# Layer 1 attention with one merged score block per unit, and its masked copies made by GpSimd

## The reference, cut to what matters

```python
qi = jnp.arange(WINDOW)[:, None] + WINDOW
kj = jnp.arange(2 * WINDOW)[None, :]
rel = qi - kj
valid = ((rel >= 0) & (rel < WINDOW))[None] & ((jnp.arange(nb)[:, None, None] > 0) | (kj[None] >= WINDOW))
scores = jnp.where(valid[None, :, None, None], scores, -jnp.inf)
m = jnp.maximum(jnp.max(scores, axis=-1), sink)
p = jnp.exp(scores - m[..., None])
denom = jnp.sum(p, axis=-1) + jnp.exp(sink - m)
o = jnp.einsum('bnhgqk,bnkhd->bnhgqd', p, vv.astype(F32)) / denom[..., None]
```

## Time and profile before

| | us |
|---|---|
| median of 3 runs | 2116.43 (2115.18 to 2119.19) |
| span of the profiled execution | 2115.3 |
| mean granted TensorE clock | 0.990 |
| busy: PE | 2045.7 (97%) |
| busy: DVE, ACT, POOL | 1604.8, 1361.3, 277.7 |
| stretch of the attention units | about 1226 to 1462 |

### The profile page before, as it was taken

How to read it: one execution, slowest core, us unless ns; L and a number is a source line. 1 busy time by engine, 2 the same in 40 slices (tenths; PEclk the granted TensorE clock), 3 DMA queues, 4 the chain that set the end, 5 groups by cost and what they waited for, 6 DMA issues and landing times. The chain is left out here.

```text
span 2115.3 us, 30221 instructions
## 1 busy us (share of the span) xinstructions
PE 2045.7 (97%) x10536; PEld 1661.4 (79%) x10536; DVE 1604.8 (76%) x2000; ACT 1361.3 (64%) x1794; POOL 277.7 (13%) x334
## 2 busy tenths in 40 slices
PE   8999998998999999999999989999899999999998
PEld 6888876787788888888877856777688888888885
DVE  4551246777888888888886267887898888888886
ACT  5333426653788887878772266675577778888774
POOL 2000000001111121111203320110111111122210
PEclk9999999999999999999999999999999999999999
DMA  4112222215999999999983020011699999999996
GB/s 139 40 60 90 78 72 78 81 65 205 343 381 390 389 389 385 380 378 380 385 317 132 1 90 11 21 61 61 231 383 380 381 384 384 387 388 385 384 363 254
DMA packets 123491, 513.28 MB, mean 243 GB/s; under 512 B 27373, under 2 KB 28490, under 8 KB 89610
## 3 DMA queue, kind: packets, MB, share of 16 engines
q1 hardware_dynamic: 103674, 474.11, 59.7%
q0 software_dynamic: 18576, 33.86, 4.2%
q10 hardware_dynamic: 1152, 4.19, 0.5%
HBM read 495.05 MB, written 50.86 MB: 258 GB/s over the span
## 5 line engine op out<-in xcount | busy, mean ns | idle before, releaser
L542 DVE TENSOR_TENSOR exp_w_lo<-ring_raw,first_w_hi 128x2048 fp32r<-128x2048 f32 x192 | 438.9, 2288 | 33.2 <-ACT first_w_hi L469 33.1
L542 DVE TENSOR_TENSOR exp_w_lo<-ring_raw,exp_w_hi 128x2048 fp32r<-128x2048 f32 x192 | 438.8, 2287 | 27.8 <-ACT exp_w_hi L469 27.8
L469 ACT ACTIVATE exp_w_hi<-ring_raw 128x2048 fp32r<-128x2048 f32 x192 | 367.7, 1918 | 62.1 <-PE exp_up_out L394 27.9
L469 ACT ACTIVATE first_w_hi<-ring_raw 128x2048 fp32r<-128x2048 f32 x188 | 360.7, 1919 | 62.2 <-PE exp_up_out L394 23.6
L339 POOL DMA_INDIRECT y_rows<-exp_y,base_rows_y x63 | 79.8, 1266 | 936.1 <-ACT exp_y L489 936.1
L394 PE MATMUL exp_gate_out<-exp_w_lo,exp_x_hi 128*128 128x512 f32 x512 | 201.1, 393 | 0.0
L394 PE MATMUL exp_y_out<-exp_w_lo,exp_hid_hi 128*128 128x512 f32 x512 | 200.4, 391 | 0.0
L394 PE MATMUL exp_up_out<-exp_w_lo,exp_x_hi 128*128 128x512 f32 x512 | 199.3, 389 | 0.0
L546 DVE TENSOR_TENSOR exp_x_lo<-exp_x_turned,exp_x_hi 128x1024 fp32r<-128x1024 f32 x62 | 75.9, 1224 | 51.4 <-ACT exp_x_hi L473 51.4
L394 PE MATMUL exp_gate_out<-first_w_hi,exp_x_hi 128*128 128x512 f32 x272 | 109.7, 403 | 3.1 <-issue 2.0
L350 POOL DMA_INDIRECT first_x_rows<-u_rows,base_rows_u x64 | 104.9, 1639 | 58.6 <-issue 52.2
(11 more groups left out here) (529 smaller groups left out, 4671.8 us busy)
## 6 DMA issues: line engine op xcount, KB each, us to landing
ring_raw<-in_expert_w_gate_dram SPq DMA_DIRECT2D x128, 1024.0 KB, 11.1
ring_raw<-in_expert_w_up_dram SPq DMA_DIRECT2D x128, 1024.0 KB, 11.6
ring_raw<-in_expert_w_down_dram SPq DMA_DIRECT2D x128, 1024.0 KB, 11.4
l0w_raw<-in_ab_w_in_dram SPq DMA_DIRECT2D x48, 256.0 KB, 2.8
finish_y<-y_rows SPq DMA_DIRECT2D x8, 1024.0 KB, 12.4
ring_raw<-in_swa_w_qkv_dram SPq DMA_DIRECT2D x5, 1024.0 KB, 10.1
ring_raw<-y_rows SPq DMA_DIRECT2D x10, 512.0 KB, 4.9
base_h<-in_x_dram ACTq DMA_DIRECT2D x8, 512.0 KB, 7.0
```

The lines of the kernel that those rows point to most:

```text
L469: nc.scalar.activation(split[split_slot(unit)][0][:], raw[raw_slot(unit)][:], ACT.Copy).then_inc(hi_ready, 1)
L542: nc.vector.tensor_tensor(lo[:], raw[raw_slot(unit)][:], hi[:].bitcast(F32), ALU.subtract).then_inc(lo_ready[split_slot(unit)], 1)
```

## The change

1. **One block of scores.** For n >= 1 ACT copies the own block's scores to `masked` (`copy_own`), and DVE overwrites the places k > q with the previous block's scores by a predicated copy. Each query so has 128 scores, not 256. Maxima, exponents and both normalizations work on 128 columns a head. For n = 0 DVE still adds a mask.
2. **Four transposes.** `turn(G)` transposes 4 blocks instead of 8; `turned` has two halves, used in turn.
3. **A copy and two masked copies.** `copy_turned(G)` writes 512 columns to `bare` in SBUF. GpSimd multiplies them by the two triangles in `band` into the two halves of `prob_t` (`band_probs(G)`, previous first), and `weigh(G)` waits for these. The wait for `out_ready` moves from ACT to GpSimd.
4. **Order.** `units` puts one output unit ahead of each turn and three behind it. On ACT `copy_own(G + 2)` comes first in a pass and `norm_even(G + 1)` right behind `copy_turned(G)`. On DVE `denominators(G + 1)` comes before `mask(G + 2)`. On GpSimd `rotate(7)`, the router's multiply and the inverse roots stand between the `band_probs`.

```diff
+            def band_probs(G):
+                pool.wait_ge(s["bare_copied"], G + 1)
+                if G >= 1:
+                    pool.wait_ge(s["out_ready"], G)
+                for b in range(0 if G >= GROUPS else 1, 2):
+                    g.tensor_tensor(by_head(prob_t[:, b * BANK:(b + 1) * BANK]), by_head(bare[G % 3]), bc(c["band"][:, b], 1, PER), ALU.mult).then_inc(s["own_made" if b else "prev_made"], 1)
...
-            for u in range(T - 2):
-                inverse_root(u)
+            for G in range(LAST):
+                band_probs(G)
+                if G == 0:
+                    rotate(T - 1)
+                    pool.wait_ge(s["router_ready"], 32)
+                    g.tensor_tensor(router[:], router[:], bc(c["ffn_gain1"], 2, 36), ALU.mult).then_inc(s["router_scaled"], 1)
+                if G % GROUPS == 0 and G >= 2 * GROUPS:
+                    inverse_root(G // GROUPS - 2)
...
-                p_of = heads4(masked[G % 3])
-                for b in range(0 if n else 1, 2):
-                    if b == 0 and G > GROUPS:
-                        pe.wait_ge(s["early_copied"], G - GROUPS)
-                    if b == 1 and G > 0:
-                        pe.wait_ge(s["prob_copied"], G)
-                    for i in range(PER):
-                        last = nc.tensor.transpose(turned[:, PER * b + i], p_of[:, i, b], c["ident"][:])
-                    last.then_inc(s["prob_turned" if b else "early_turned"], 1)
+                if G > 1:
+                    pe.wait_ge(s["bare_copied"], G - 1)
+                for i in range(PER):
+                    last = nc.tensor.transpose(turned_at(G)[:, i], by_head(masked[G % 3])[:, i], c["ident"][:])
+                last.then_inc(s["prob_turned"], 1)
...
                     if b == 0:
-                        pe.wait_ge(s["early_copied"], G - GROUPS + 1)
+                        pe.wait_ge(s["prev_made"], G - GROUPS + 1)
                     else:
-                        pe.wait_ge(s["prob_copied"], G + 1)
+                        pe.wait_ge(s["own_made"], G + 1)
...
-            units = {(0, 0): (0, 3), (0, 1): (3, 4), (1, 0): (4, 7), (1, 1): (7, 8), (2, 0): (8, 9), (2, 1): (9, 10), (3, 0): (10, 14), (3, 1): (14, 16)}
+            units = {(0, 0): (0, 1), (0, 1): (1, 4), (1, 0): (4, 5), (1, 1): (5, 8), (2, 0): (8, 9), (2, 1): (9, 12), (3, 0): (12, 13), (3, 1): (13, 16)}
...
+            def copy_own(G):
+                act.wait_ge(s["scored"], G + 1)
+                act.wait_ge(s["prob_turned"], G - 2)
+                a.activation(by_head(masked[G % 3]), heads4(scores)[:, :, 1], ACT.Copy).then_inc(s["own_copied"], 1)
+
             def copy_turned(G):
-                if G >= 1:
-                    act.wait_ge(s["out_ready"], G)
...
+                act.wait_ge(s["prob_turned"], G + 1)
+                if G >= 3:
+                    act.wait_ge(s["own_made"], G - 2)
+                a.activation(by_head(bare[G % 3]), turned_at(G), ACT.Copy).then_inc(s["bare_copied"], 1)
...
+                    dve.wait_ge(s["own_copied"], G - GROUPS + 1)
+                    v.copy_predicated(by_head(masked[j]), bc(c["tri_strict"][:].bitcast(U32), 1, PER), heads4(scores)[:, :, 0]).then_inc(s["masked_made"], 1)
```

More of the change, by code:

```diff
@@ L2297, in layer1 @@
         q_cols, prob_t = [chunks(work[j][:]) for j in range(2)], work[2][:]
-        masked = [work[n][:] for n in (3, 4, 5)]
+        masked, bare = [work[n][:, 0:BANK] for n in (3, 4, 5)], [work[n][:, BANK:] for n in (3, 4, 5)]
+        turned_at = lambda G: turned[:, PER * (G % 2):PER * (G % 2 + 1)]
         r_rows = [q[:, t + 2, 0:1024] for t in range(5)] + [raw_ring[4][:, 0:1024], late[:, 1], late[:, 2]]
@@ L2824, in exponents @@
             def exponents(G):
-                j, first = G % 3, 0 if G >= GROUPS else P
+                j = G % 3
                 act.wait_ge(s["tops_made"], G + 1)
                 for i in range(PER):
-                    span = slice(i * 2 * P + first, (i + 1) * 2 * P)
-                    a.activation(masked[j][:, span], masked[j][:, span], ACT.Exp, bias=neg_top[j][:, i:i + 1], accum_out=total[j][:, i:i + 1])
+                    own = by_head(masked[j])[:, i]
+                    a.activation(own, own, ACT.Exp, bias=neg_top[j][:, i:i + 1], scale=HEAD_DIM ** -0.5, accum_out=total[j][:, i:i + 1])
@@ L2830, in exponents @@
                 a.activation(sink_part[j][:], sink_part[j][:], ACT.Exp).then_inc(s["prob_made"], 1)
             def norm_even(G):
-                j, first = G % 3, 0 if G >= GROUPS else P
+                j = G % 3
                 act.wait_ge(s["inv_made"], G + 1)
                 for i in range(2):
-                    span = slice(i * 2 * P + first, (i + 1) * 2 * P)
-                    last = a.activation(masked[j][:, span], masked[j][:, span], ACT.Copy, scale=inv[j][:, i:i + 1])
+                    own = by_head(masked[j])[:, i]
+                    last = a.activation(own, own, ACT.Copy, scale=inv[j][:, i:i + 1])
@@ L3023, in denominators @@
                 for i in range(2, PER):
-                    span = slice(i * 2 * P + first, (i + 1) * 2 * P)
-                    last = v.tensor_scalar(masked[j][:, span], masked[j][:, span], inv[j][:, i:i + 1], None, ALU.mult)
+                    own = by_head(masked[j])[:, i]
+                    last = v.tensor_scalar(own, own, inv[j][:, i:i + 1], None, ALU.mult)
                 last.then_inc(s["odd_normed"], 1)
```

56 lines of the change are left out of this document (24 added, 32 removed).

## The result

The changed kernel takes 2182.52 us in the median (2179.62 to 2187.34), the kernel before on the same chip 2117.26. The ratio is 1.0306, with a 95% interval of 1.0293 to 1.0319: slower by 65 us, where 2173 us was forecast, with 2140 to 2200 as the range. The profiled execution spans 2177.9 us against 2115.3, so 62.6 us are to be found. Of all executions on record one, of experiment 7, ran in a slow state and took 3930 us; it is left out of the ratios but not out of that kernel's median.

What follows compares the result with a forecast made beforehand. PE was taken to bound the kernel before, the chain through ACT and GpSimd the changed one. Terms 31 + 2.6 + 3 + 2 + 12 + 6 = 57 us on 2115.3 gave 2172, plus 1.1 against the median 2173 us; range 2140 to 2200.

Steps and rivals of the forecast that it cites:

- (a): On PE: four transposes fewer a unit, 0.39 us each in 28 units, 11 us in all while PE bounds.
- (b): Chain from one weighing to the next through ACT and GpSimd's pair: 6.9 us in an ordinary unit.
- (c): Units of a block from n = 2 on: 7.4, 11.6, 8.9 and 6.9 us, together 31 us more for five blocks.
- (d): Other units: +2.6 us for units 4 to 8, +3 for n = 0, +2 for the last block.
- (e): PE's clock falls after the long waits in g = 1, slowing the next stretch: 0 to 18 us, +12 taken.
- (f): SBUF port shared by DVE and GpSimd: instructions hold each other, +6 us, with 0 and 25 as ends.
- PE stays the bound: Rival: both masked copies done 2.6 us after the turn, so PE gains its 11 us; 2108 us, chance 4 in 100.
- Only the inverse root bites: Rival: GpSimd's pair runs in about 1.8 us and only g = 1 loses, some 4 us a block; about 2138, chance 11.
- The port decides: Rival: DVE's short steps hold most pairs by 0.9 us, with the full clock loss; about 2198 or more, chance 10.
- Nothing moves: Rival: gain and waits cancel, time within 0.2%; chance 3.

Runs made afterwards that it cites:

- experiment 7: Changed kernel with both masked copies on DVE straight from PSUM, without ScalarE's copy and GpSimd's pair; 2119.35 us, ratio 1.0005.
- experiment 2: Changed kernel with 44 transposes of the identity on PE ahead of the weighing of g = 1 from block 2 on; 2167.05 us, ratio 1.0234.
- experiment 1: Changed kernel with GpSimd's inverse root one unit later, behind the masked copies of g = 1; 2158.92 us, ratio 1.0189.
- experiment 6: Changed kernel with all four heads normalized by ScalarE and none by DVE; 2188.93 us, ratio 1.0324.
- experiment 5: Changed kernel with the inverse root one unit later and 16 transposes of the identity in the gap left; 2153.22 us, ratio 1.0169.
- experiment 8: Changed kernel with one masked copy in place of two, using differences of V, and the inverse root at g = 1; 2117.29 us, ratio 0.9997.
- experiment 10: Kernel with one masked copy a unit and output unit 8 moved to g = 1, plus ScalarE normalizing all four heads; 2114.95 us, ratio 0.9986.
- experiment 3: Changed kernel with GpSimd multiplying two heads of four in each masked copy; 2162.84 us, ratio 1.0217.

## Why the prediction was right, and where it was off

The direction, the place and the size came out. Step by step:

- **(a) PE gives up its bound.** Right: from 141.92 us busy to 116.21 in the same stretch. Experiment 7 shows the gain of the four transposes on PE, 8.0 us in 20 units; it also shows that this gain is not worth its time by itself, since PE then waits for DVE's copies.
- **(b) The chain of an ordinary unit, 6.9 us.** Measured 6.94 or 6.95 in each g = 3 of blocks 2 to 6. All terms stand in the timelines: exponents 0.54 behind `out_high`, 1.64 for five of them, `copy_own` 0.48, the copy 0.58, the pair 2.50. The pair had been bounded by 2.4 and 3.1; the row of 1.287 was the right one to be near, and 1.267 is the median.
- **(c) g = 0, 1, 2.** The values 7.4, 11.6 and 8.9 were measured as 7.43 (blocks 2 and 3), 11.6 to 12.2 and 8.5 to 8.95, the last two where experiment 2 kept the clock up. Experiment 1 confirms the queue of GpSimd as the cause of g = 1. That g = 2 hangs on the late turn is read from ScalarE's wait for it; no run moved the router's product. From unit 8 to 28 the chip took 45.2 us more, of which experiment 2 gives 11.0 to the clock and leaves 34.2. The prediction had 31 for it, and 10 of the clock.
- **(d) Other units.** Units 4 to 8 cost 3.4 where 2.6 was forecast. For 4, 6, 7 and 8 the steps hold (8.1, 8.1, 8.1 and 7.4 against 7.9, 8.0, 8.0, 7.4). Unit 5 takes 9.04 and not 7.9: DVE has a weight copy there, and steps of it that GpSimd holds, and the exponents wait for DVE; with DVE's multiplies gone (experiment 6) it takes 7.87. **For n = 0 the step failed in size:** 5.4 us and not 3. Unit 1 costs 2.6, as worked out. Units 2 and 3 were given 0.2 each, since they "lose the normalization and one weight copy from the chain"; they cost 1.25 and 1.55. No weight copy left the chain. Before and after, one of 0.95 us stands ahead of the copy of the turned block, and only the normalization (0.6) has moved behind, while `copy_own` (0.48), a hand-over and the masked copy (1.28) came in. ScalarE's timeline shows that order in the changed kernel:

```profile
1252.90 0.20 ACT L2837 ACTIVATE l_sink_part<-l_sink_part 128x4 f32<-128x4 f32 x1
1252.99 1.05 ACT L2829 ACTIVATE l_w_hi<-l1r_w_raw 128x1024 fp32r<-128x1024 f32 x1
1253.94 0.59 ACT L2850 ACTIVATE l_work<-l_wide 128x512 f32<-128x512 f32 x1
1254.42 0.59 ACT L2856 ACTIVATE l_work<-l_turned 128x512 f32<-128x512 f32 x1
```

  Units 29 to 31 cost 6.9, where 2 and 2 of the clock were forecast; by experiment 2 it is 2.9 and 4.0 of the clock. Their g = 1 and g = 2 are long like those of the other blocks (12.42 and 11.08), and before only g = 2 was.
- **(e) The clock.** 12 us forecast, 15 measured by experiment 2. The range of 0 to 18 held. One number in its working was misread: the 0.76 is GpSimd's busy time in the earlier trace rows, and the clock of those 2 us was 0.61. The clock so was low from about 1242.4, for 6.8 us and not 6, which makes 3.4 a unit of the highest loss in place of 3. That it came near 2 each was in part luck: the step had no way to choose between 0 and 3, the low stretch is 6 us long in some units and 13 in others, and it doesn't take a gap of 4.5 us to bring it on: in experiment 1 the clock goes after 1.58 and 0.48.
- **(f) The port.** The size came out, the way to it did not. It acts on DVE and not on GpSimd: none of the 60 masked copies took over 1.46 us, so no pair was held by 0.89, from which the 7 us were worked out. Most of DVE's holds lie beside the chain, as was said. Experiment 6, which takes DVE's multiplies away, shortens g = 0 of blocks 4 to 7 by 0.3 to 0.55 us, unit 5 by 1.2, and g = 1 of blocks 4 to 6 by 0.35 to 0.4 and of block 7 by 1.0: some 5 us in all against the 6. That is the holds together with the multiplies' own 0.48 us. An example from DVE's and GpSimd's timelines of the changed kernel, where the multiplies take 0.48 us when nothing runs beside them:

```profile
1415.39 2.49 POOL L2483 TENSOR_TENSOR l_work<-l_work,base_band 128x512 f32<-128x512 f32 x2 [5.47 <-ACT l_work L2856]
```

```profile
1415.68 2.29 DVE L3036 TENSOR_SCALAR l_work<-l_work,l_inv 128x128 f32<-128x128 f32 x2
1417.89 0.72 DVE L3017 COPY_PREDICATED l_work<-base_tri_strict,l_wide 128x512 f32<-128x512 uint32 x1
```

  Both end within 0.1 us of each other (1417.88 and 1417.97). The Trainium skill (SBUF — State Buffer, "Who interferes with whom") says of a DVE instruction that uses both of its port pairs that whoever issues first has the shared pair for the whole instruction and the other fully blocks. This trace agrees for DVE, and of the other order, a GpSimd copy held by DVE, it has 0.2 us at most. The copy that reads its data from PSUM (L3017) took 0.72 us each time, between the bounds of 0.58 and 1.29 that stood for it.

Of the rivals, "PE stays the bound" is ruled out by PE's 116.21 us busy, and by g = 3, which is the chain's length to 0.05 us. "Only the inverse root bites" was the nearest in its mechanism; with the inverse root elsewhere and the clock kept (experiment 5) 36 of the 65 us are still there. "The port decides" needed pairs that DVE holds by 0.9 us, and there are none; experiment 6 leaves some 5 us for the port. That its kernel is no faster is no argument, since the clock took those back. "Nothing moves" is ruled out by the ratio.

The sum, in the prediction's order, forecast against measured: 31 and 34.2 for the blocks without the clock, 2.6 and 3.4, 3 and 5.4, 2 and 2.9, 12 and 15.0, and 6 in (f), which is no term of its own in the measured sum, since its 5 us lie within the others, in the blocks and in unit 5 above all. The terms measured add up to 60.9, and 0.5 ahead of the attention and 1.2 behind it make the 62.6.

Left open: where all of the 2.7 us behind the attention in experiment 8 and the 4.5 in experiment 7 go (PE's waits there show 1.4 and 1.5 of them), and why blocks 1 and 7 are longer in experiment 10.

## What to carry to other kernels

Before work is taken from the engine that bounds a stretch, write down the chain that runs beside it from one of its waits to the next; here it was 6.9 us long beside some 6.7 that PE's work would have been. An engine that had been busy for a tenth of the time, and now is for a third, became part of the limit because its two instructions stood in series. Work the chain out for each kind of unit and not for the ordinary one alone: g = 3, with nothing added, lost no time, and the loss lies in the units where one more copy, a late turn or another job of an engine stands in the chain. Look through the in-order queue of the engine that gets the work: what stood there for nobody in the units (4.6 us of small steps) is ahead of one of them in each block now. When the work can't be moved without a wait, change what has to be made: one masked copy in place of two, by a difference of the other operand and together with the root moved by a unit, took back all 65 us (as did the copies on a faster engine in experiment 7), where experiments 1 to 6 took back 29 at most.

## What the runs showed of the hardware

- **The clock falls after short idle stretches too.** In experiment 1 two of 1.58 and 0.48 us, 0.65 us apart, were followed by 0.50. Before the change a wait of 0.2 to 0.3 us now and then left it at 1.00 for the whole stretch.
- **It doesn't come back after an equal time.** In the changed kernel the clock was low for some 6 us in blocks 3 to 6 and for 13 us in block 2, with PE busy in both:

```profile
1314.00:1316.00 2.00, 0.92 (x4) 0.33 (x4) 0.00 (x0) 0.00 (x0) 2.00 (x2) 0.57 0.00 0
...
1318.00:1326.00 8.00, 8.00 (x32) 6.72 (x33) 4.64 (x10) 2.90 (x13) 0.00 (x0) 0.50 0.16 66
1326.00:1328.00 2.00, 2.00 (x6) 1.58 (x5) 0.00 (x0) 1.02 (x3) 1.48 (x2) 0.52 0.00 0
1328.00:1330.00 2.00, 2.00 (x13) 1.04 (x13) 0.00 (x0) 0.00 (x0) 1.04 (x1) 1.00 0.00 0
```

  The long form costs some 3 us more a unit (12.34 against 9.4 in g = 2). It came in one block of the changed kernel, and g = 2 is that long in three blocks of experiment 3 and in four of experiment 6, two and three more. That is 7 us of the 14 by which experiment 3 missed its forecast, and 10 of the 12 of experiment 6. What decides between the two I can't say. Experiment 6 shortened the chain by half a microsecond in some units and lost 10 us by it, so kernels with such gaps are compared by units at full clock, or with the gaps filled as in experiment 2.
